# Down-projection as seven block products in place of eight, with block sums on GpSimd and VectorE

## The reference

```python
    x = x + jnp.concatenate([out_a, out_d], axis=-1) @ w_out
    h = rms_norm(x, mlp_norm)
    x = x + jnp.square(jax.nn.relu(h @ w_up)) @ w_down
```

## Time and profile before

| | us |
|---|---|
| median of 3 runs | 635.77 |
| lowest, highest | 634.98, 635.86 |
| profiled execution, its time | 634.36 |
| its span, first to last instruction | 632.5 |
| granted clock of PE, mean | 0.995 |

### The profile page before, as it was taken

The page is one execution under the profiler, slowest core; times in us unless marked ns, Lnnn a source line. Parts: engine busy times, 40 slices in busy tenths (PEclk is TensorE's granted clock), DMA queues, the critical chain, the costliest instruction groups (busy, mean ns, idle before and its releaser), DMA issues.

```text
span 632.5 us, 10515 instructions
## 1 busy us (share of the span) xinstructions
PE 614.5 (97%) x3673; PEld 532.7 (84%) x3673; DVE 384.8 (61%) x606; ACT 300.7 (48%) x500; POOL 48.0 (8%) x46
## 2 busy tenths in 40 slices
PE   6999999999999999999989999999999999999995
PEld 5787787899899898998867787788999898998983
DVE  3864665588565655656268555757975555755643
ACT  3755466655433524434175555664652533425312
POOL 1420130010000000000004101300100000000001
PEclk8999999999999999999999999999999999999999
DMA  8953234328746465463237334332676456465201
GB/s 306 321 190 116 95 135 133 124 78 275 258 147 238 145 193 204 144 248 139 68 128 269 117 108 179 85 117 67 207 264 225 169 171 226 136 220 176 99 0 66
DMA packets 58659, 104.18 MB, mean 165 GB/s; under 512 B 1744, under 2 KB 34816, under 8 KB 58624
## 3 DMA queue, kind: packets, MB, share of 16 engines
q1 hardware_dynamic: 57712, 102.31, 48.1%
q10 hardware_dynamic: 912, 1.43, 0.6%
HBM read 102.69 MB, written 1.05 MB: 164 GB/s over the span
## 4 chain that ended last, share of the span: by engine, by line
PE 87%; issue 4%; DVE 3%; POOL 3%; ACT 2%; ACTq 0%; POOLq 0%; DVEq 0%
PE bank L753 27%; PE bank L755 26%; PE bank L754 26%; PE bank L823 2%; PE bank L760 1%; POOL roped L327 1%; PE bank L840 1%; PE bank L839 1%; PE bank L859 1%; PE bank L838 1%; PE bank L855 1%; PE bank L814 1%; POOL rope_r L338 1%; ACT w_hi L376 1%; DVE w_lo L510 1%
## 5 line engine op out<-in xcount | busy, mean ns | idle before, releaser
L510 DVE TENSOR_TENSOR w_lo<-raw,w_hi 128x1024 fp32r<-128x1024 f32 (+1 forms) x192 | 232.0, 1245 | 54.5 <-ACT w_hi L376 54.5
L376 ACT CAST w_hi<-raw 128x1024 fp32r<-128x1024 f32 x192 | 193.2, 1050 | 23.1 <-PE bank L755 13.2
L753 PE MATMUL bank<-xt_hi,w_hi 128*128 128x256 f32 x512 | 144.8, 283 | 0.0
L755 PE MATMUL bank<-xt_hi,w_lo 128*128 128x256 f32 x512 | 144.7, 283 | 0.0
L754 PE MATMUL bank<-xt_lo,w_hi 128*128 128x256 f32 x512 | 144.5, 282 | 0.0
L458 ACT CAST h_hi<-up_sq 128x512 fp32r<-128x512 f32 x32 | 19.9, 622 | 186.8 <-DVE up_sq L657 186.8
L753 PE MATMUL bank<-w_hi,h_hi 128*128 128x512 f32 x256 | 101.4, 396 | 0.0
L754 PE MATMUL bank<-w_lo,h_hi 128*128 128x512 f32 x256 | 101.2, 396 | 0.0
L755 PE MATMUL bank<-w_hi,h_lo 128*128 128x512 f32 x256 | 101.2, 395 | 0.0
L754 PEld LDWEIGHTS bank<-xt_lo,w_hi 128*128 128x128 f32 x512 | 97.9, 191 | 1.4
L753 PEld LDWEIGHTS bank<-xt_hi,w_hi 128*128 128x128 f32 x512 | 97.9, 191 | 1.3
(11 more groups left out here) (86 smaller groups left out, 634.0 us busy)
## 6 DMA issues: line engine op xcount, KB each, us to landing
raw<-in_w_up SPq DMA_DIRECT2D x32, 1024.0 KB, 5.6
...
raw<-in_w_in SPq DMA_DIRECT2D x4, 512.0 KB, 5.6
x<-in_x SPq DMA_DIRECT2D x1, 512.0 KB, 4.6
x<-in_x ACTq DMA_DIRECT2D x1, 512.0 KB, 7.9
final_gain<-in_final_norm SPq DMA_DIRECT2D x1, 512.0 KB, 5.6
```

Source lines behind the costliest of these rows:

```text
L376: act.copy(w_hi[:, slot, part], raw[:, slot, part]).then_inc(hi_done, 1)
L510: dve.tensor_tensor(w_lo[:, slot, part], raw[:, slot, part], w_hi[:, slot, part].bitcast(F32), ALU.subtract).then_inc(split_done, 1)
L753: pe.matmul(out, s_hi, m_hi, start=first, stop=False)
L755: return pe.matmul(out, s_lo, m_hi, start=False, stop=last)
```

## The change

For 15 of the 16 slices of each layer (all but the last) the down-projection, seen as a product of 2 x 2 blocks, is made by a scheme of seven products (Strassen's in Winograd's form). With A[t][j] the blocks of h (128 x 128) and B[j][n] those of w_down (128 x 512), the seven are A11 B12, A12 B22, S4 B21, A22 T4, S1 T1, S2 T2 and SN TN, where SN = A21 - A11, S1 = A21 + A22, S2 = A22 + SN, S4 = A12 - S2 and T1 = B11 - B12, TN = B11 - B21, T2 = B12 - TN, T4 = B22 - T2. Each accumulates over the 15 slices in a bank of its own (p1 to p7), so the combination of the seven to the four output blocks is made once per layer. The seven banks and one bank for the up-projection (`up_bank`; before there were two) are all of PSUM.

- POOL makes the T sums of each chunk out of `raw` by three instructions of 1024, 512 and 512 columns, into one of two buffers (in `roped` and `v`), as soon as the weights have landed and DVE's t_lo of two slices before is done. ACT then makes `t_hi` (2048 columns, in `ot_hi`) and DVE `t_lo`; there is one buffer of each.
- DVE makes the S sums by four instructions of 128 columns, from SBUF to SBUF. ReLU and square move from DVE to ACT. h_hi and h_lo have seven blocks (896 columns) in place of four.
- Of a fast down chunk only three quarters (B12, B21, B22) go through w_hi and w_lo, in one instruction each in place of two.
- PE: `down` does three products from w, waits for t_lo, and does four from T. `up` waits for the ReLU of the slice before.
- SP reloads a down chunk's slot only when POOL's sums are done.
- At the end of the layer ACT copies p1 and p5, DVE and POOL form u2 to u5 from the banks and add them to x, while PE does the last slice in the old way (`down_last`) into p3, p2, `up_bank` and p4. Then the four additions to x follow as before. `final_gain` lies in the place of `k_t` and is loaded when POOL's last addition is done.

```diff
-SPLIT_TURNS = MLP_TURNS - 1
+FAST = UPS - 1
+A12, A22, A11, A21 = 4, 5, 6, 7
+S_N, S_1, S_2, S_4 = 0, 1, 2, 3
+T_1, T_N, T_2, T_4 = 0, 1, 2, 3
...
+        up_bank = banks[4]
+        up_0 = [banks[5], banks[6]]
+        p1, p2, p3, p4, p5, p6, p7 = banks[0], banks[1], banks[2], banks[3], banks[5], banks[6], banks[7]
+        acc_y = [[p3, p2], [up_bank, p4]]
...
+            sp.wait_ge(x_pool_added, 2 * DEPTH)
             sp.dma_start(final_gain[:, :], final_g.rearrange("(a n) -> a n", a=1).broadcast_to([P, D_MODEL]))\
...
+                def t_sum(l, i, slot, b, seen):
+
+                    wait_all(pool, (raw_ready[slot], seen), (t_split, l * FAST + i + 1))
+                    b11, b12 = raw[:, slot, 0:BANK], raw[:, slot, BANK:2 * BANK]
+                    b22 = raw[:, slot, 3 * BANK:4 * BANK]
+                    both = raw[:, slot, BANK:3 * BANK].rearrange("p (u c) -> p u c", u=2)
+                    ts = t_sums[b]
+                    pool.tensor_tensor(ts[:, T_1:T_N + 1, :], b11.unsqueeze(1).broadcast_to([P, 2, BANK]), both,
+                                       ALU.subtract).then_inc(t_step, 1)
+                    pool.wait_ge(t_step, l * (2 * FAST) + i * 2 + 1)
+                    pool.tensor_tensor(ts[:, T_2, :], b12, ts[:, T_N, :], ALU.subtract).then_inc(t_step, 1)
+                    pool.wait_ge(t_step, l * (2 * FAST) + i * 2 + 2)
+                    pool.tensor_tensor(ts[:, T_4, :], b22, ts[:, T_2, :], ALU.subtract).then_inc(t_summed, 1)
...
+                pool.wait_ge(p_scaled, l * 2 + 1)
+                pool.tensor_tensor(x[:, 0, BANK:2 * BANK], x[:, 0, BANK:2 * BANK], r_c1, ALU.add)\
+                    .then_inc(x_pool_added, 1)
+                wait_all(pool, (u_done, 1), (u_done, l * 3 + 1), (p_copied_5, l + 1))
+                pool.tensor_tensor(u4, u2, c5, ALU.add).then_inc(u_pool_done, 1)
+                pool.wait_ge(p_scaled, l * 2 + 2)
+                pool.tensor_tensor(x[:, 1, BANK:2 * BANK], x[:, 1, BANK:2 * BANK], r_u3, ALU.add)\
+                    .then_inc(x_pool_added, 1)
...
+                def t_to_hi(l, i, c, b):
+
+                    wait_all(act, (t_summed, FAST), (t_summed, l * FAST + i + (1 + FAST)),
+                             (weights_used, l * UNITS + c * 2 + 6))
+                    act.copy(t_hi[:, :, :], t_sums[b]).then_inc(t_hi_done, 1)
+
+                def period(l, i, b, tiles, c_up, seen_up, seen_down):
+
+                    relu_square(l, i, tiles, c_up)
+                    up_slot, down_slot = (3, 0) if b == 0 else (1, 2)
+                    hi(l, c_up_next(i), up_slot, 0, seen_up)
+                    h_to_hi(l, i, b)
+                    hi(l, c_up_next(i), up_slot, 1)
+                    hi_fast(l, i * 2 + (FIRST_UP + 4), down_slot, seen_down)
+                    t_to_hi(l, i, i * 2 + (FIRST_UP + 2), b)
...
+                act.wait_ge(weights_used, used(l, 2 * (CHUNKS - 2) + 1))
+                act.copy(c1, p1[:, :]).then_inc(p_copied_1, 1)
+                act.copy(c5, p5[:, :]).then_inc(p_copied_5, 1)
+                act.wait_ge(rstd_done, l * STATS + ST_M + 1)
+                act.activation(r_c1, p1[:, :], ACT.Copy, scale=rstd[:, ST_M, 0:1]).then_inc(p_scaled, 1)
+                act.wait_ge(u_done, l * 3 + 2)
+                act.activation(r_u3, u3, ACT.Copy, scale=rstd[:, ST_M, 1:2]).then_inc(p_scaled, 1)
...
+                def h_sums(l, i):
+
+                    step = l * (2 * FAST) + i * 2 + 1
+                    dve.wait_ge(squared, l * UPS + i + 1)
+                    dve.tensor_tensor(hs[:, S_N, :], hs[:, A21, :], hs[:, A11, :], ALU.subtract).then_inc(s_step, 1)
+                    dve.tensor_tensor(hs[:, S_1, :], hs[:, A21, :], hs[:, A22, :], ALU.add)
+                    dve.wait_ge(s_step, step)
+                    dve.tensor_tensor(hs[:, S_2, :], hs[:, A22, :], hs[:, S_N, :], ALU.add).then_inc(s_two, 1)
+                    dve.wait_ge(s_two, l * FAST + i + 1)
+                    dve.tensor_tensor(hs[:, S_4, :], hs[:, A12, :], hs[:, S_2, :], ALU.subtract).then_inc(s_step, 1)
...
+                def period(l, i, b):
+
+                    up_slot, down_slot = (3, 0) if b == 0 else (1, 2)
+                    h_sums(l, i)
+                    lo(l, i * 2 + (FIRST_UP + 3), up_slot, 0)
                     h_to_lo(l, i, b)
+                    lo(l, i * 2 + (FIRST_UP + 3), up_slot, 1)
+                    lo_fast(l, i * 2 + (FIRST_UP + 4), down_slot)
+                    t_to_lo(l, i, b)
...
+                dve.tensor_tensor(u2, p6[:, :], c1, ALU.add).then_inc(u_done, 1)
+                dve.wait_ge(u_done, l * 3 + 1)
+                dve.tensor_tensor(u3, p7[:, :], u2, ALU.add).then_inc(u_done, 1)
+                dve.wait_ge(u_done, l * 3 + 2)
+                dve.wait_ge(p_copied_5, l + 1)
+                dve.tensor_tensor(u5, u3, c5, ALU.add).then_inc(u_done, 1)
                 dve.wait_ge(rstd_done, l * STATS + ST_M + 1)
+                dve.wait_ge(u_pool_done, l + 1)
+                add_to_x(u4, 0, 0, ST_M, x_based)
+                dve.wait_ge(u_done, l * 3 + 3)
+                add_to_x(u5, 1, 0, ST_M, x_based)
+                dve.wait_ge(x_based, l * 2 + 2)
...
             def down(l, i, c, slot, b, first=False, last=False):
...
+                pe.wait_ge(h_split, l * UPS + i + 2)
+                unit_ready(l, c, 1)
+                for bank, a, u in ((p1, A11, 1), (p2, A12, 3), (p3, S_4, 2)):
+                    cols = slice(u * BANK, (u + 1) * BANK)
+                    mm = product(l, bank, b, a, w_hi[:, slot, cols], w_lo[:, slot, cols], first,
+                                 last and bank is p1)
+                mm.then_inc(weights_used, 1)
+                pe.wait_ge(t_split, l * FAST + i + 3)
+                for bank, a, u in ((p4, A22, T_4), (p5, S_1, T_1), (p6, S_2, T_2), (p7, S_N, T_N)):
+                    mm = product(l, bank, b, a, t_hi[:, u, :], t_lo[:, u, :], first, last and bank is not p4)
+                mm.then_inc(weights_used, 1)
```

More of the change, by code:

```diff
@@ L284, in load_down @@
                     src = down_v[bass.ds(l, 1), :, bass.ds(i * 2, 2), :]
-                    load(l, c, slot, src.rearrange("a p k n -> p (a k) n"), 2)
+                    load(l, c, slot, src.rearrange("a p k n -> p (a k) n"), 2,
+                         sums=l * FAST + i + (FAST - 1) if slot != 3 else None)
                 load_up(l, FIRST_UP, 0, FIRST_UP % RING)
@@ L454, in h_to_hi @@
                 def h_to_hi(l, i, b):
-                    act.wait_ge(h_done, l * UPS + i + 1)
+                    wait_all(act, (s_step, 1), (s_step, l * (2 * FAST) + i * 2 + 2))
                     act.wait_ge(weights_used, used(l, i * 4 + (2 * (FIRST_UP - 2) + 1)))
-                    act.copy(h_hi[:, b, :, :], up_sq[:, :].rearrange("p (a b) -> p a b", a=2))\
-                        .then_inc(h_hi_done, 1)
-                def hi_chunk(l, c, slot, seen):
-                    for half in range(2):
-                        hi(l, c, slot, half, seen if half == 0 else None)
@@ L475, in _, with hi_fast @@
-                h_to_hi(l, UPS - 3, 1)
-                for c in (CHUNKS - 3, CHUNKS - 2):
-                    hi_chunk(l, c, c % RING, visit(l, c))
-                h_to_hi(l, UPS - 2, 0)
-                hi_chunk(l, CHUNKS - 1, (CHUNKS - 1) % RING, visit(l, CHUNKS - 1))
-                h_to_hi(l, UPS - 1, 1)
+                    act.copy(h_hi[:, b, :, :], hs[:, 0:7, :]).then_inc(h_hi_done, 1)
+                def hi_fast(l, c, slot, seen):
+                    wait_all(act, (raw_ready[slot], seen), (weights_used, l * UNITS + c * 2 + 2))
+                    act.copy(w_hi[:, slot, BANK:4 * BANK], raw[:, slot, BANK:4 * BANK]).then_inc(hi_done, 2)
@@ L688, in _, with lo_fast @@
-                square_relu(l, UPS - 1, [banks[5][:, :]], CHUNKS - 3)
-                h_to_lo(l, UPS - 1, 1)
-                dve.wait_ge(rstd_done, l * STATS + ST_M + 1)
+                def lo_fast(l, c, slot):
+                    dve.wait_ge(hi_done, l * UNITS + c * 2 + 2)
+                    part = slice(BANK, 4 * BANK)
+                    dve.tensor_tensor(w_lo[:, slot, part], raw[:, slot, part],
+                                      w_hi[:, slot, part].bitcast(F32), ALU.subtract).then_inc(split_done, 2)
@@ new lines, in _ @@
+                for half in range(2):
+                    lo(l, FIRST_UP + 1, (FIRST_UP + 1) % RING, half)
+                lo_fast(l, FIRST_UP + 2, (FIRST_UP + 2) % RING)
+                with dve.Fori(0, MLP_TURNS) as j:
+                    for b in range(2):
+                        period(l, j * 2 + b, b)
+                h_sums(l, UPS - 2)
+                lo(l, CHUNKS - 1, 3, 0)
+                h_to_lo(l, UPS - 2, 0)
+                lo(l, CHUNKS - 1, 3, 1)
+                t_to_lo(l, FAST - 1, 0)
@@ new lines, in up, with product @@
+                        if f == 0 and k == 0 and i is not None:
+                            pe.wait_ge(relu_done, l * UPS + i)
```

(23 more changed lines are left out.)

166 lines of the change are left out of this document (92 added, 74 removed).

## The result

| | before | after |
|---|---|---|
| median of 4 runs, us | 635.53 | 692.05 |
| lowest, highest | 634.98, 635.86 | 690.18, 692.88 |
| span of the profiled execution | 632.5 | 690.7 |
| granted clock of PE, mean | 0.995 | 0.965 |

The ratio is 1.089 (95% interval 1.087 to 1.090): 56.5 us slower. The forecast was 718.6, with a range of 690 to 748.

A forecast was written before the change was run, and what follows sets the result against it. PE was taken to bound the old kernel, DVE and POOL taking turns the new. 634.4 us profiled + 72.2 in both layers' MLPs + 10.6 tails = 717.2; 1.4 to the median gave 718.6, range 690 to 748.

The forecast's parts named there:

- part-overlap rival: In the MLP, POOL holds the port only while it reads: period near 11.8 us, total 680 us; chance 0.08.
- What PE gains: Fast down chunks: seven products instead of eight save 0.70 us each, 21.0 us in all; PE's period falls to 10.66.
- The step that decides: In each MLP period, POOL's SBUF-reading sums and DVE's two-SBUF-input instructions fully exclude each other: 8.0 + 4.8 = 12.8 us minimum.
- No exclusion: Rival: POOL's sums run beside DVE in the MLP, PE's 10.66 us period holds, total 629 us; chance 0.07.
- The period: Steady MLP period of 13.3 us: 12.8 held by DVE and POOL, 0.5 of waits for ACT; bounds 12.4 and 14.3.
- Start: MLP start: first t_lo ends 20.1 us after U, the end of the first up chunk.
- a clock below 0.9 in the stage: Sign in the MLP stage named as showing the forecast wrong; it expected granted clock 1.00 there.
- Tail: Layer ends: last addition at E+10.6, E being the last fast chunk's end, 4.25 us later than before; tails cost 10.6 us.
- The signs named beforehand: MLP: POOL's 512-column sums 2 us or more, DVE's 128-column sums over 1 us, periods 13.3, PE share 0.84, clock 1.00.
- PE's clock: Rival: PE's clock falls in its MLP waits; with half the work at 1.2 GHz, period 16 us, total 789; chance 0.07.

The follow-up runs named there:

- seven_only: Changed kernel without T sums, t_hi and t_lo; four products multiply w_down blocks instead, so the output is not the reference's: 623.0 us, 0.981 of before.
- before_pool: Kernel before, plus eight unread 512-column subtractions on POOL per MLP slice, for which no other engine waits: 695.8 us, one run.
- before_pool_writes: Kernel before, plus eight 512-column memsets on POOL per MLP slice, each behind a two-column subtraction: 635.2 us, one run.
- t_on_dve: Changed kernel with the T sums moved from POOL to DVE, between its w_lo and t_lo: 661.1 us, 1.041 of before.
- start_early: Changed kernel with T sums on DVE, t_hi and t_lo before three-quarter w_hi and w_lo, first chunk's sums on POOL before the MLP: 634.2 us.
- before_pool_four: Kernel before, plus four 512-column subtractions of two different tensors on POOL per MLP slice: 657.4 us, 1.035 of before.
- seven_pool: Changed kernel without t_hi and t_lo, POOL's T sums made but unread, output not the reference's: 643.5 us, 1.012 of before.

## Why the forecast was right, point by point

The time, 692.05, lies in the range but 2 us from its lower end, as the period does (12.44, with 12.4 as its lower bound). By the total alone it is nearer to the 680 of the part-overlap rival than to 718.6; the parts below are what speaks for the forecast.

**What PE gains.** Right: 0.69 us per chunk, period 10.65 (seven_only).

**The step that decides.** Right in kind, a little too strong. The exclusion read from rows 6 holds in the new stage for DVE's 128 and 896 columns beside POOL's 512 and 1024 (third and fourth h sum, h_lo), it acts with nobody waiting for POOL (before_pool), and not for instructions without SBUF input (before_pool_writes). "No exclusion" falls with that. A part overlap as the forecast priced it, 1.5 us per period, isn't there either: POOL's 512-column sums still hold DVE for 1.05 and 0.95 us. But "full exclusion for the whole of each instruction" goes too far: POOL's three sums hold DVE for 4.2 us, where the forecast had 4.8 and their durations with DVE out of the way are 2.40, 1.29 and 1.28.

**The period.** 13.3 forecast, 12.44 measured: the term that was mis-sized. By its own parts: DVE 8.0 forecast, and the same rows without POOL add up to 8.2 (t_on_dve's rows, less T sums and waits for ACT). POOL 4.8 forecast, 4.2 measured, being 2.2 + 1.05 for the two sums in front of the third and fourth h sum and 0.95 for the one in front of h_lo: the rest of their durations runs beside DVE. Waits for ACT 0.5 forecast, none measured: the layout had all of POOL's sums in front of the fourth h sum, but the third came beside w_lo, so h_hi, w_hi and t_hi on ACT were ready while DVE waited for POOL. 26 periods at 0.86 are 22 us of the 26.5 by which the time was missed (measured, the 13 periods behind the first t_lo take 162.3 us in layer 0, 10.6 less than forecast).

**Start.** First t_lo's end 20.1 us behind U forecast, 18.7 measured (161.65 against 142.9). The kind was right (the sums of two chunks and six DVE instructions in turns), but the forecast gave PE's waits no effect on the clock, and there was one: 0.50 in 151 to 164, which is the forecast's own sign of being wrong, a clock below 0.9 in the stage. It cost little here, since DVE set the pace: DVE waits once for the slower PE by way of ACT's square, 0.70 us, at 174.71. From the end of the 14th t_lo to the end of the fast chunks are 13.7 us, where 13.5 was forecast.

**Tail.** The last addition to x was forecast at E+10.6 and ended at E+11.0. The rows, beside those of rows 8 and 9 (ACT's copy of p1 starts as E is reached, at 337.7):

```profile
337.77 0.59 ACT L578 COPY rope_a<-bank 128x512 f32<-128x512 f32 x1 [2.90 <-PE bank L887]
```

```profile
340.76 1.74 POOL L404 TENSOR_TENSOR q_t<-rope_b,rope_a 128x512 f32<-128x512 f32 x1
...
342.61 3.35 DVE L635 SCALAR_TENSOR_TENSOR x<-q_t,rstd,x 128x512 f32<-128x512 f32 x2 [1.26 <-POOL q_t L404]
346.00 2.73 DVE L635 SCALAR_TENSOR_TENSOR x<-bank,rstd,x 128x512 f32<-128x512 f32 x4
349.41 0.48 DVE L621 SCALAR_TENSOR_TENSOR xt_lo<-bank,gains,xt_hi 128x256 fp32r<-128x256 f32 x1 [0.69 <-ACT xt_hi L443]
...
684.12 0.69 DVE L842 TENSOR_TENSOR rope_a<-x,k_t 128x512 f32<-128x512 f32 x1
...
679.58 0.35 SPq L330 DMA_DIRECT2D k_t<-in_final_norm  x1
```

The four last additions (2.73 us together) stand close behind the two of u4 and u5 (3.35 us, one drawn out by POOL's last addition, the other by POOL's w_lo, which the forecast had at no cost), and u4 on POOL took 1.74 us behind u5. Here two more steps failed. The 2.56 us at the loop's end were taken as added behind the last addition; the gap in front of xt_lo is now 0.69 and its cause is ACT's xt_hi. PE's first product came 12.2 us behind E, where before has 9.5, so 2.7 later and not 4.25; the rest of the boundary's 3.7 fits the clock, which is 0.50 from 345.4 to 352.2, around PE's wait of 4.2 us. That 3.7 is close to 4.25 is luck. And final_gain did not hold up the end: issued at 679.58, it landed after 3.8 us, not the 5.6 of rows 9, before DVE wanted it at 684.12. The end is 4.0 longer, not 6.4.

**The signs named beforehand.** PE waits for t_lo, POOL's third sum takes over 2 us and the clock in the stage's middle is 1.00, as named. Others were off: the t_lo are 12.4 us apart and not 13.3, POOL's second sum takes 1.29 (it is DVE that waits there), only two of the four h sums wait for POOL, the clock was 0.50 at the start, and PE's busy share is 0.89, not 0.84, as it has 12.44 us and not 13.3 to wait in and ran partly at 1.2 GHz.

**The rivals.** PE's clock: in the steady periods PE waits 1.5 us in each 12.4 and the granted clock stays 1.00. In the stretch 151 to 164 it is 0.50 where PE waited for 6.9 us, 0.74 where it waited for 5.4 and 0.87 for 3.5, so the rival's place was the start, not the period. The length of one wait doesn't settle it: behind the 2.5 us of start_early came half the clock, and the 3.0 us of before and 2.8 of before_pool_four (at 159.9, clock 1.00 in 157 to 165) left it at 1.00. The Trainium skill ("TensorE: Matmul & The Clock Gate", HAM oscillation) has it that idle gaps between bursts bring the clock down; these rows agree for the long waits and show that the short ones of each period don't. What the fall costs depends on who sets the pace: 0.7 us here, about 3 per layer in seven_pool.
